# Compression weights in units used one after the other, resident tile constants, and a later place for the last quarter's pair ranking in a two-layer decoder kernel

## What is computed

```python
def compress(t, pe, w1, w2):                      # once for k, once for v
    blk = t[:, cidx] + pe[None, None, :, None, :]
    ...
    return jax.nn.gelu(blk @ w1) @ w2             # w1: 2048 x 256

s_half = jnp.einsum('thpc,pnc->thpn', q, sub_keys)   # 8 heads x 2 halves x 128
v_half, i_half = lax.top_k(s_half, 16)
cand = (v_half[:, :, 0, :, None] + v_half[:, :, 1, None, :])   # 16 x 16 pairs
top_s, top_pos = lax.top_k(cand, 16)
expert_idx = jnp.take_along_axis(cand_idx, top_pos, axis=-1)
gate = jax.nn.softmax(top_s, axis=-1)
act = jax.nn.gelu(jnp.einsum('cd,chkd->chk', hc, u[ic]))
out = jnp.einsum('chk,chkd->cd', gc * act, v[ic])     # 128 experts a token
```

## Time and profile before

| what | value |
|---|---|
| median of 3 runs | 1766.62 us |
| the profiled execution's own time | 1769.09 us |
| its span, first to last instruction | 1767.2 us |
| mean granted TensorE clock | 0.870 of full |
| busy: PE, DVE, ACT, POOL | 1350.6, 1095.5, 515.4, 663.3 us |
| read from memory over the span | 686.68 MB |

### The profile page before, as it was taken

One profiled execution on the slowest core, in us unless ns is written; L12 is line 12 of the kernel. 1 busy time (PEld: TensorE's weight loads), 2 busy tenths in 40 slices (PEclk: granted clock), 3 DMA queues, 4 the chain that ended last, 5 costly groups with the idle time before them and its releaser, 6 DMA issues. The chain is left out here.

```text
span 1767.2 us, 22780 instructions
## 1 busy us (share of the span) xinstructions
PE 1350.6 (76%) x8310; PEld 692.7 (39%) x8310; DVE 1095.5 (62%) x2746; ACT 515.4 (29%) x1295; POOL 663.3 (38%) x1028
## 2 busy tenths in 40 slices
PE   8999886679999857666888776777888865655556
PEld 5855842245564623222354443233354531111111
DVE  5510588984334859778434757797554868965444
ACT  3411232362212222226232222225342322221112
POOL 0000234344333425335434334343443445565551
PEclk9999988789999979778989888877999877687787
DMA  9755599999999999999999999999999999999996
GB/s 386 294 172 181 216 421 421 414 393 422 395 421 421 420 420 416 421 371 420 421 421 422 421 421 420 421 393 401 411 420 421 421 419 393 422 412 421 422 421 276
DMA packets 96160, 690.28 MB, mean 391 GB/s; under 512 B 11056, under 2 KB 11184, under 8 KB 12720
## 3 DMA queue, kind: packets, MB, share of 16 engines
q0 software_dynamic: 73728, 536.90, 73.6%
q1 hardware_dynamic: 22320, 151.92, 21.4%
HBM read 686.68 MB, written 2.10 MB: 390 GB/s over the span
## 5 line engine op out<-in xcount | busy, mean ns | idle before, releaser
L524 POOL DMA_INDIRECT uv_rows<-uv_in,idx x512 | 503.7, 984 | 1062.0 <-PE acc_pe L1308 825.1
L1308 PE MATMUL acc_pe<-uv_rows,diag 64*64 64x512 f32 x4096 | 623.0, 738 | 314.3 <-ACT diag L1037 299.7
L569 DVE CUSTOM_DVE_ANT_0 uv_rows<-uv_rows,h_ps 128x1024 f32<-128x1024 f32 x512 | 607.0, 1218 | 240.3 <-DMA uv_rows<-uv_in,idx 228.2
L1308 PEld LDWEIGHTS acc_pe<-uv_rows,diag 64*64 64x64 f32 x4096 | 156.0, 156 | 688.5 <-ACT diag L1037 470.1
L1030 ACT ACTIVATE gelu_b<-act_b,h_scale 128x2 f32<-128x2 f32 x255 | 75.1, 294 | 746.8 <-DVE act_b L569 741.5
L1362 PE MATMUL bank<-w_own,h_t 128*128 128x512 f32 x384 | 175.3, 610 | 3.1 <-ACTq L1078 3.0
L1338 PEld LDWEIGHTS bank<-h_t,w_own 128*128 128x128 f32 x1504 | 169.8, 192 | 18.5 <-issue 18.5
L1338 PE MATMUL bank<-h_t,w_own 128*128 128x128 f32 x1504 | 173.9, 276 | 0.0
L518 POOL TENSOR_TENSOR diag<-ident_st,gate 128x64 f32<-128x64 f32 x512 | 159.4, 312 | 9.6
L1037 ACT ACTIVATE diag<-diag,gelu_b 128x64 f32<-128x64 f32 x510 | 149.6, 340 | 8.3
L1362 PEld LDWEIGHTS bank<-w_own,h_t 128*128 128x128 f32 x384 | 73.1, 196 | 108.3 <-issue 103.8
(11 more groups left out here) (203 smaller groups left out, 1181.5 us busy)
## 6 DMA issues: line engine op xcount, KB each, us to landing
w_own<-blocks_in SPq DMA_DIRECT2D x112, 1024.0 KB, 10.6
uv_rows<-blocks_in SPq DMA_DIRECT2D x24, 1024.0 KB, 9.7
uv_rows<-uv_in,idx POOLq DMA_INDIRECT x512, 15.6
tcon<-tile_consts_in SPq DMA_DIRECT2D x4, 432.5 KB, 12.4
xs<-x_in SPq DMA_DIRECT2D x2, 512.0 KB, 14.0
uv_rows<-mem_in SPq DMA_DIRECT2D x1, 1024.0 KB, 13.8
mem_gained<-uv_rows SPq DMA_DIRECT2D x1, 1024.0 KB, 15.3
area<-mem_gained SPq DMA_DIRECT2D x1, 1024.0 KB, 8.4
```

The costliest lines, as they stand in the source:

```text
L524: nc.gpsimd.indirect_dma_start(uv_rows[:, slot_of(k, earlier), :, :].rearrange("p a n -> p (a n)"), None, a["uv"], bass.IndirectOffsetOnAx ...
L569: v.tensor_tensor_reduce(u_row, u_row, h_ps[:, :], 1.0, 0.0, ALU.mult, ALU.add, act_b[:, k // B % AHEAD, k % B:k % B + 1]).then_inc(sems[" ...
L1308: mm = pe.matmul(acc_pe[c * HT:(c + 1) * HT, r * BLK:(r + 1) * BLK], diag[tok, slot_of(k), :], uv_rows[tok, slot_of(k), 1, c * BLK:(c + 1) ...
```

## The change

Three things:

1. **Compression weights in turn.** The two matrices are laid out again as `cmp0` and `cmp1`, whose four units each hold a quarter of the depth of *both*. The product works through them in four quarters, and each of the first three lets its unit go by an increment of `half_used`.
2. **Constants resident.** One array of 960 columns serves both tiles and is loaded in the first stage only. The history of the convolution is a zero fill or a copy instead of a product with a flag, and the pooling of a first tile has 16 columns of its own.
3. **Order.** In `PLAN` and `MEM_PLAN`, `rank_pairs3`, `rank_pairs_more3`, `look_up3`, `look_up_more3` and `gates3` go from between `turn_kv` and `cmp_in` to between `mix_turn` and `xq1`. The sums of quarter 3 go to `area1`.

```diff
-for _name, _w in (("causal", S), ("cadd", NC), ("cvalid", NC), ("cur", 4 * P), ("prev", 4 * NC), ("flag", 1)):
+for _name, _w in (("causal", S), ("cadd", TILES * NC), ("cvalid", TILES * NC), ("cur", 4 * P), ("prev", 4 * NC),
+                  ("early", 4 * NC)):
...
-    ("ck", 0): ("HID", False), ("cv", 0): ("HID", False), ("ck", 1): ("HID", True), ("cv", 1): ("HID", True),
+    ("cmp0", 0): ("HID", False), ("cmp0", 1): ("HID", False), ("cmp1", 0): ("HID", False), ("cmp1", 1): ("HID", True),
...
-        "look_up2", "look_up_more2", "zk2", "rope", "rank3", "rank_more3", "turn_kv", "rank_pairs3",
-        "rank_pairs_more3", "branch_gates", "gates2", "gates3", "look_up3", "look_up_more3", "cmp_in", "cmp_hidden",
+        "look_up_more2", "zk2", "rope", "rank3", "rank_more3", "turn_kv", "branch_gates", "gates2", "cmp_in",
...
+        "win_values0", "win_values1", "win_out", "small_branches", "mix_turn", "rank_pairs3", "wo0",
+        "rank_pairs_more3", "wo1", "look_up3", "xa_norm", "look_up_more3", "xq0", "gates3", "xq1", "xa_scores",
...
-            half_jobs = [job for job in jobs if any(freed_by[u] == (job, False) for u in units)]
-            half_no = {job: i + 1 for i, job in enumerate(half_jobs)}
+            freed_within = [u for job in jobs for u in units if freed_by[u] == (job, False)]
+            half_no = {u: i + 1 for i, u in enumerate(freed_within)}
...
-                        sp.dma_start(tcon[:, :], a["tile_consts"][bass.ds(tile, 1), :, :].rearrange(
-                            "a p n -> (a p) n")).then_inc(sems["tile_consts_loaded"], 16)
+                        sp.dma_start(tcon[:, :], a["tile_consts"]).then_inc(sems["tile_consts_loaded"], 16)
...
-                    if dense is not None and not first:
-                        load_tile_consts()
-
...
-                        step(v.tensor_scalar(hc[:, :, 0:HIST], hc[:, :, P:P + HIST], tile_const("flag"), None,
-                                             ALU.mult))
+                        if own_half:
+                            step(v.memset(hc[:, :, 0:HIST], 0.0))
+                        else:
+                            step(v.tensor_copy(hc[:, :, 0:HIST], hc[:, :, P:P + HIST]))
...
+                        late = q == 3 and dense is not None
+                        sums = (area1[:, 1024:1536] if late else area3[:, q * BLK:(q + 1) * BLK]).rearrange(
+                            "p (h i j) -> p h i j", h=2, i=TOPK)
...
-                        for half in range(2):
-                            w = [need_unit(name, half) for name in ("ck", "cv")]
-                            for i in range(4 * half, 4 * half + 4):
+                        for n in range(4):
+                            w = need_unit(f"cmp{n // 2}", n % 2)
+                            for i in range(2 * n, 2 * n + 2):
                                 for part in range(4):
                                     kind, c = part // 2, 2 * i + part % 2
                                     mm = pe.matmul(out[part * 32:part * 32 + 32, 0:CMP_HIDDEN],
-                                                   cmp_in[:, kind, c, :], w[kind][:, c - 8 * half, :],
+                                                   cmp_in[:, kind, c, :], w[:, 4 * kind + c - 4 * n, :],
                                                    start=(i == 0), stop=(i == 7))
-                            if half == 0:
+                            if n < 3:
                                 mm.then_inc(sems["half_used"], 1)
```

More of the change, by code:

```diff
@@ L143 @@
+            "cmp_in", "cmp_hidden", "cmp_hidden_turn", "conv0", "conv1", "cmp_kv", "conv2", "conv3", "cmp_scores",
             "sel_scores", "sel_more", "sel_exps", "cmp_probs", "conv4", "conv5", "cmp_out", "sel_turn", "win_scores",
             "win_more", "win_exps", "conv6", "conv7", "sel_values0", "sel_values1", "sel_out", "conv_norm",
[L145 to L146 removed]
@@ L1695, in constants, with put @@
     t = np.arange(P)
[L1696 to L1698 removed]
+    tile_consts = np.zeros((P, N_TC), np.float32)
+    def put(name, value):
         at, w = TC[name]
[L1700 to L1718 removed]
+        tile_consts[:, at:at + w] = value
+    later = P + t
+    put("causal", np.where(np.arange(S)[None, :] <= later[:, None], 0.0, NEG))
+    n = np.arange(NC)
+    ok = np.stack([(n[None, :] * CMP_STRIDE + CMP_BLOCK - 1 <= tile * P + t[:, None]) & (n[None, :] < N_CMP)
+                   for tile in range(TILES)], 1)
+    put("cadd", np.where(ok, 0.0, NEG).reshape(P, -1))
+    put("cvalid", ok.reshape(P, -1))
+    cur, prev, early = np.zeros((P, 4, P)), np.zeros((P, 4, P)), np.zeros((P, 4, NC))
+    for g, w in enumerate(POOL_WINDOWS):
+        for o in range(P):
+            for i in range(P + o + 1 - w, P + o + 1):
+                (cur if i >= P else prev)[i % P, g, o] = np.float32(1.0 / w) - (1.0 if i == P + o else 0.0)
+        for o in range(NC):
+            start = max(o + 1 - w, 0)
+            early[start:o + 1, g, o] = np.float32(1.0 / (o + 1 - start))
+            early[o, g, o] -= 1.0
+    put("cur", cur.reshape(P, -1))
+    put("prev", prev[:, :, :NC].reshape(P, -1))
+    put("early", early.reshape(P, -1))
     head_mask = (t[:, None] // NC == np.arange(HEADS)[None, :]).astype(np.float32)
@@ L1735, in put_block @@
             rows = columns(w)
-            if name in COLS_BLOCKS and name not in ("ck", "cv"):
+            if name in COLS_BLOCKS:
                 rows = rows.reshape(P, KC, 2, BLK // 2).transpose(0, 2, 1, 3)
@@ L1750 @@
         put_block("ab", w_in[:, 1304:1816])
-        put_block("ck", given["cmp_w1"][l, 0])
-        put_block("cv", given["cmp_w1"][l, 1])
+        w1 = np.stack([columns(given["cmp_w1"][l, kind]).reshape(P, 4, 4, CMP_HIDDEN) for kind in range(2)], 2)
+        for i in range(2):
+            blocks[l * len(WHERE) + WHERE[f"cmp{i}"]] = w1[:, 2 * i:2 * i + 2].reshape(P, -1)
         for name, w, n in (("wo", given["w_out"][l], 2), ("xq", given["xa_wq"][l], 2), ("xo", given["xa_wo"][l], 2),
```

72 lines of the change are left out of this document (27 added, 45 removed), and 14 rows, old and new, of tables (MEM_PLAN, PLAN).

## The result

| | median, us | lowest to highest | runs |
|---|---|---|---|
| before | 1765.78 | 1761.28 to 1769.22 | 19 |
| changed | 1773.86 | 1765.66 to 1777.93 | 19 |

The ratio is 1.0037, 95% interval 1.0027 to 1.0046: **slower**, by little but clear of the noise, 6.5 us by the ratio and 8.1 us by the medians, where 15 us less were forecast. The median lies outside the range of 1744.5 to 1762. The single times say more than the median: 5 of the 19 lie at 1765.7 to 1769.4, 14 at 1771.6 to 1777.9, while those of before are one heap, 8 us wide. The profiled execution is one of the five (1765.86 us, span 1764.1).

What follows compares the result with a forecast made beforehand. Behind the first stage, DMA bytes at 421 GB/s plus holes without DMA work were taken to set the time. Savings of 3.0 + 5.0 + 7.0 = 15.0 us from 1766.6 gave 1751.6 us, range 1744.5 to 1762.

Steps and rivals of the forecast that it cites:

- Bytes: Constant loads: three fewer in stages 1 to 3, one slightly larger in the first stage, net 3.0 us less.
- lower bound of 0: Constant loads: no gain from fewer bytes if the loads stand ahead of a hole that only computing sets.
- I take the upper end because the holes should close: Constant loads: reason for taking 3.0 us between bounds of 0 and 3.2.
- Compression in turn: Stage 2 compression: shorter PE block and earlier weight refill nearly close a 5.4 us DMA hole; 5.0 us, bounds 2.6 and 5.4.
- one wait near 9: Sign at stage 2's compression: PE's block takes about 11 to 12 us, with a single such wait in its last quarter.
- No window under 300 GB/s behind it: Sign behind stage 2's compression block: DMA rate stays at or above this value.
- Quarter 3 later: Stages 1 and 3: less DVE work ahead of compression shrinks holes there and in the attention; 7.0 us, bounds nothing and 10.0.
- the attention has one batch more for the same dense work: Stage 3 attention: 5 us more for DMA, 2.4 for DVE, so the 3.3 us hole shrinks to near nothing.
- gone or short: Sign in stages 1 and 3: what PE's wait for the compression input should become.
- at 421 through it: Sign in stages 1 and 3: DMA's rate in GB/s through PE's wait for the compression input.
- Cost where it goes: Output projections: DVE's idle time covers quarter 3's moved work, ACT idles enough for two more table loads; cost 0.
- The slower one: Rival at the projections: PE waits for DVE and ACT on the late stretch, 21 us lost, 1772.8 us; chance 0.06.

Runs made afterwards that it cites:

- e8: Resident constants alone, put into the kernel before, with compression in halves and the old order: 1765.94 us, ratio 0.9990.
- e11: Compression in turn alone, put into the kernel before, with constants loaded for each tile and the old order: 1761.98 us, ratio 0.9973.
- e4: The changed kernel with its compression weights in halves again, as before; constants resident, new order: 1772.62 us, ratio 1.0034.
- e2: The changed kernel with the two plans and the place of the sums as before; constants and compression as changed: 1762.40 us, ratio 0.9985.
- e5: The changed kernel with its new order, but as many batches behind each step as the old lists gave: 1757.01 us, ratio 0.9947.
- e12: The kernel of new order and old batch counts, measured again on another chip: 1758.00 us, ratio 0.9945.
- e1: The changed kernel again without any edit, profiled in a slower execution: 1772.96 us, ratio 1.0041.
- e15: The changed kernel with old batch counts in stage 1 and the attention of stages 2 and 3, not beside the output projection: 1757.55 us, ratio 0.9952.

## Why the prediction was wrong

- **Bytes (3.0 us).** The bytes were right, 685.40 MB. The time was not: e8 gives 1.8 us at an interval of -0.4 to 3.7, and beside e11 the pair gains nothing more. Alone, e8 can't tell the forecast 3.0 from the term's lower bound of 0; beside the compression in turn the record speaks for the lower bound. "I take the upper end because the holes should close" borrowed from another term, whose holes did not close.
- **Compression in turn (5.0 us).** Right in size in the kernel before: 4.8 us (e11), and in the trace 12.3 us of block against 11.1 to 12.0, the hole behind it mostly closed. In the changed kernel it was not to be seen at the end (e4). The sign was wrong: "one wait near 9" forgets that by the prediction's own sum two quarters, 1.8 us, are worked inside the landing time of 9.3, which leaves 7.5. That is what e11 shows, at full clock:

```profile
755.59 2.80 PE L1465 MATMUL bank<-w_own,area 128*32 128x256 f32 x48 [0.82 <-DVE area L724]
765.84 1.93 PE L1465 MATMUL bank<-w_own,area 128*32 128x256 f32 x16 [7.45 <-DMA w_own<-blocks_in]
```

In the changed kernel the wait was 5.03 us, as PE did the first 48 matmuls at half clock (5.35 us) and so spent more of the landing time on work; that time itself is some 8.6 us, an estimate from the block's start and a third of 5.35 us. "No window under 300 GB/s behind it" holds for the 2 and 8 us shown; single microseconds go down to 270 and 279.
- **Quarter 3 later (7.0 us, bounds 0 to 10).** This is the step that failed. With the counts of before it gains 4 to 5 us by the medians and 7 by the ratios (e2 against e5 and e12), near the forecast, and the two windows lose 8.1 us less than before and 5.9 less than e2. In the changed kernel's trace the hole ahead of the compression in stage 3 is halved (378 GB/s from 1135 to 1150 us, 1.5 us for 3.0), and the one in the attention grows. As the change has it, it costs 10 us (e2 against e1), since the counts that it moves cost 14 to 16. The words at fault: "the attention has one batch more for the same dense work, 5 us more for DMA and 2.4 for DVE, so the hole of 3.3 us should shrink". The batch more stands there only as far as the window's scores in stages 2 and 3 (9 for 8); over the whole attention the number is the same, and in stage 1 it is the same even so far. And it is a sum over a stretch. Where within it the batches stand decides, by e5 against e1, and I never looked where the rounding would put them; the lower bound of nothing was argued, though PE's clock of 0.75 stood in the very row quoted for it, and a loss was not allowed at all. A sign failed too: PE's wait for the compression input was to be "gone or short" and is 4.97 us in stage 1 (3.82 before) and 3.16 in stage 3 (1.19 before), which fits the batch between the gates and that input that went as well. It is hardly a part of the loss, for e12 waits there too, 3.12 and 3.16 us. DMA "at 421 through it" came true in stage 1 (419 to 422 GB/s from 305 to 335 us) and not in stage 3 (the 378 above).
- **Cost where it goes (0).** Right: DVE's idle times took it, POOL waited for no gates of quarter 3, PE's new pause of 3.81 us left DMA at 419 GB/s, and e15 shows that even the batches there may shift by one without any effect.
- **The rivals.** The slower one gave 1772.8 us, and 1773.9 was measured, but for a wrong reason: it put 21 us on the output projection, where nothing is lost. That it came within 1.1 us is luck. None of the rivals was a counter of batches that moves, although the change rewrites the list from which it is worked out. What stays open is which shift of stage 1 carries its 9 us, and by what pause or clock the shifts cost what they cost.

The best kernel of the study is e5: the whole change with the old counts, 1757 to 1758 us, 0.55% under before by its ratios (0.9947 and 0.9945).

## What to carry to other kernels

Where a planner gives out background work in proportion, an edit of its list is two edits: the order, and every rounding behind it. Print the counts of both versions step by step, and try the new order with the old counts before judging it. And a sum of work over a stretch does not tell how its pieces are spread: here the same number of batches, spread otherwise by single steps, cost 14 to 16 us, though no single pause could be named for it.

## What the runs showed of the hardware

- After a pause of PE of 5.67 us one execution of the changed kernel has the clock back within some 5 us, and another, of the same instructions, stays at 1.2 GHz for 15 us. The times of this kernel lie in two groups some 8 us apart, and each of the two profiles belongs to one; e5, with other counts of batches, has one group, 1.3 us wide.
- DMA sets the time of this kernel, yet PE's clock shows in it, since PE frees the slots: in those 15 us at half clock DMA moved 320, 349 and 51 GB/s, where in the other execution it moved 423, 415 and 413 in the same three windows.
